# The low halves of 18 weight panels computed on GpSimd instead of VectorE

## What is computed

```python
def swiglu(x, w_in, w_out):
    g, u = jnp.split(x @ w_in, 2, axis=-1)
    return (jax.nn.silu(g) * u) @ w_out

def hgrn2_mixer(x, w_in, gnorm_w, w_out, lb):
    q, f_pre, i_in, g = jnp.split(x @ w_in, ...)     # 1024 -> 4096
    ...                                              # gated recurrence by blocks of 16
    return o.reshape(B, S, D_MODEL) @ w_out
# diff_attention: x @ w_in is 1024 -> 3072; pool_mixer: 1024 -> 1024;
# hybrid_mixer: 1024 -> 5656; recurrent_mixer: 1024 -> 2048
```

## Time and profile before

| what | before |
|---|---|
| median of 3 runs | 3395.22 us (3392.09 to 3395.25) |
| the profiled execution | 3390.7 us |
| its span, first to last instruction | 3389.0 us |
| mean granted TensorE clock | 0.968 |
| TensorE busy | 3157.4 us (93%) |
| VectorE busy | 2276.0 us (67%) |
| ScalarE busy | 1741.2 us (51%) |
| GpSimd busy | 183.0 us (5%) |

### The profile page before, as it was taken

The page is one execution under the profiler, slowest core; times in us unless marked ns, Lnnn a source line. Parts: engine busy times, 40 slices in busy tenths (PEclk is TensorE's granted clock), DMA queues, the critical chain, the costliest instruction groups (busy, mean ns, idle before and its releaser), DMA issues.

```text
span 3389.0 us, 43988 instructions
## 1 busy us (share of the span) xinstructions
PE 3157.4 (93%) x17560; PEld 2714.7 (80%) x17560; DVE 2276.0 (67%) x2669; ACT 1741.2 (51%) x2101; POOL 183.0 (5%) x147
## 2 busy tenths in 40 slices
PE   8998999998899998899998899999897999997798
PEld 7876888887688887788886788888675888886687
DVE  7667585857476776575857667575865675857674
ACT  5555554645454654554645555554443554644553
POOL 1010000001000101001000000101000101000000
PEclk9998999999899999999998999999897999998899
DMA  5542354553245454354553245454430454553353
GB/s 205 192 155 105 121 193 178 183 190 137 87 172 189 173 187 162 121 190 162 199 187 124 100 149 191 170 190 170 149 137 1 154 195 162 199 187 119 117 187 124
DMA packets 74056, 534.72 MB, mean 158 GB/s; under 512 B 8336, under 2 KB 8464, under 8 KB 9104
## 3 DMA queue, kind: packets, MB, share of 16 engines
q1 hardware_dynamic: 73872, 532.07, 44.1%
HBM read 530.99 MB, written 1.05 MB: 157 GB/s over the span
## 4 chain that ended last, share of the span: by engine, by line
PE 74%; DVE 12%; ACT 6%; DVEq 5%; issue 1%; DMA 0%; ACTq 0%; SPq 0%
PE pp L1840 35%; PE pp L1841 17%; PE pm L1840 8%; PE pp L1963 4%; PE pm L1841 4%; DVE wlo L1667 3%; ACT whi L1512 2%; DVE h L1695 2%; DVEq L1694 2%; PE pp L1862 2%; DVE mix L1693 1%; ACT corr L1569 1%; DVEq L375 1%; DVE mix L1792 1%; PE pp L1864 1%
## 5 line engine op out<-in xcount | busy, mean ns | idle before, releaser
L1840 PE MATMUL pp<-xs,whi 128*128 128x512 f32 x4912 | 1741.9, 400 | 27.7 <-DVE tsum L1712 25.0
L1667 DVE TENSOR_TENSOR wlo<-raw,whi 128x2048 fp32r<-128x2048 f32 x485 | 1110.3, 2292 | 461.2 <-ACT whi L1512 461.1
L1841 PE MATMUL pp<-xs,wlo 128*128 128x256 f32 x4912 | 1376.9, 280 | 0.0
L1840 PEld LDWEIGHTS pp<-xs,whi 128*128 128x128 f32 x4912 | 933.3, 190 | 256.4 <-issue 39.6
L1512 ACT ACTIVATE whi<-raw 128x2048 fp32r<-128x2048 f32 x485 | 925.0, 1911 | 289.6 <-DMA raw<-weights 288.8
L1841 PEld LDWEIGHTS pp<-xs,wlo 128*128 128x128 f32 x4912 | 936.0, 191 | 0.7 <-issue 0.2
L1569 ACT ACTIVATE corr<-pp 128x512 f32<-128x512 f32 x356 | 211.5, 594 | 561.4 <-PE pp L1841 535.8
L1712 DVE TENSOR_TENSOR tsum<-pp,corr 128x512 f32<-128x512 f32 x343 | 236.5, 690 | 314.9 <-ACT corr L1569 314.2
L1840 PE MATMUL pp<-hs,whi 128*128 128x512 f32 x1120 | 395.8, 394 | 0.0
L1840 PE MATMUL pm<-hs,whi 128*128 128x512 f32 x1120 | 393.0, 392 | 0.0
L1488 POOL TENSOR_TENSOR mix<-mix 128x512 f32<-128x512 f32 (+1 forms) x126 | 178.8, 1419 | 3189.2 <-ACT mix L1538 2914.9
(11 more groups left out here) (339 smaller groups left out, 2464.8 us busy)
## 6 DMA issues: line engine op xcount, KB each, us to landing
raw<-weights SPq DMA_DIRECT2D x505, 1024.0 KB, 4.8
h<-x_by_feature SPq DMA_DIRECT2D x1, 1024.0 KB, 6.9
out<-h SPq DMA_DIRECT2D x4, 256.0 KB, 2.5
vec<-vectors SPq DMA_DIRECT2D x1, 264.0 KB, 7.3
lamrow<-diff_lambda SPq DMA_DIRECT2D x1, 128.0 KB, 14.7
skiprow<-ssm_d SPq DMA_DIRECT2D x1, 8.0 KB, 14.6
```

The costliest lines, as they stand in the source:

```text
L1667: v.tensor_tensor(wlo[:, slot, :], raw[:, slot, :], whi[:, slot, :].bitcast(F32), ALU.subtract).then_inc(sem("weights_lo"), 1)
L1840: mm(bank, whi[:, slot, c:c + P], x_k, start=start, stop=False)
L1841: return mm(bank[:, 0:T], wlo[:, slot, c:c + P], x_k[:, 0:T], start=False, stop=stop)
```

## The change

GpSimd makes the low part of panels 5, 8, 11, 14 and 17 of each mixer, counted from 0 at its first panel, as far as they belong to an input projection. That is 18 panels: four in each HGRN mixer (5, 8, 11, 14), three in differential attention (5, 8, 11), five in the hybrid mixer (5, 8, 11, 14, 17), two in the RG-LRU mixer (5 and 8), none in the pooling mixer. VectorE skips these; TensorE waits for a semaphore of their own. GpSimd's loop over the sublayers is unrolled, and the panels' subtractions stand between the sublayer's first four adds and its last three. Each waits only for `weights_hi` of its panel.

```diff
+                elif s["kind"] != FFN and not seg.wide and g - s["segs"][0].g0 in (5, 8, 11, 14, 17):
+                    pool_low_panels.add(g)
...
+        def low_parts_of(pe, g):
+
+            if g in pool_low_panels:
+                pe.wait_ge(sem("pool_weights_lo"), pool_lows_before[g] + 1)
+            else:
+                pe.wait_ge(sem("weights_lo"), lows_before[g] + 1)
...
-            with pool.Fori(0, len(subs)) as n:
+            for s in subs:
+                n = s["n"]
                 for k in (2, 4, 6):
                     pool.wait_ge(sem("squares_ready"), 6 * n + k // 2)
                     add(sq[:, 0:2, :], sq[:, k:k + 2, :])
                     pool.drain()
                 add(sq[:, 0, :], sq[:, 1, :]).then_inc(sem("squares_added"), 1)
+                for seg in s["segs"]:
+                    for g in range(seg.g0, seg.g0 + seg.panels):
+                        if g in pool_low_panels:
+                            slot = g % SLOTS
+                            pool.wait_ge(sem("weights_hi"), splits_before[g] + 1)
+                            nc.gpsimd.tensor_tensor(wlo[:, slot, :], raw[:, slot, :], whi[:, slot, :].bitcast(F32), ALU.subtract
+                                                    ).then_inc(sem("pool_weights_lo"), 1)
...
             def split(g):
 
-                if g >= panels or g in whole_panels:
+                if g >= panels or g in whole_panels or g in pool_low_panels:
                     return
...
             def first_pair(seg, fill):
 
                 g = seg.g0
-                pe.wait_ge(sem("weights_lo"), splits_before[g] + 2)
+                low_parts_of(pe, g)
+                low_parts_of(pe, g + 1)
...
             def panel_product(g, half, r, between=None):
-                pe.wait_ge(sem("weights_lo"), splits_before[g] + 1)
+                low_parts_of(pe, g)
```

More of the change, by code:

```diff
@@ L95, in build @@
     splits_before, whole_panels = [], set()
+    lows_before, pool_lows_before, pool_low_panels = [], [], set()
     log1ps = hgrns = seconds = 0
@@ L111, in build @@
                 splits_before.append(g - len(whole_panels))
+                lows_before.append(splits_before[-1] - len(pool_low_panels))
+                pool_lows_before.append(len(pool_low_panels))
                 if seg.whole:
                     whole_panels.add(g)
+                elif s["kind"] != FFN and not seg.wide and g - s["segs"][0].g0 in (5, 8, 11, 14, 17):
+                    pool_low_panels.add(g)
             panels += seg.panels
@@ L351, in pe_rec @@
             pe.wait_ge(sem("panel_out"), seg.r0)
-            pe.wait_ge(sem("weights_lo"), splits_before[seg.g0] + 1)
+            low_parts_of(pe, seg.g0)
             w = seg.g0 % SLOTS
@@ L1905, in down_products @@
                 for p in range(seg.wide):
-                    pe.wait_ge(sem("weights_lo"), splits_before[seg.g0 + p] + 1)
+                    low_parts_of(pe, seg.g0 + p)
                     wide_wait(p)
```

## The result

The changed kernel takes 3441.31 us (median of 4 runs, 3437.95 to 3443.89) where the kernel before takes 3395.23 (4 runs): the ratio is 1.0135, with a 95% interval of 1.0123 to 1.0147. It is slower by 46 us, where 37 were forecast; the time lies inside the range. Its profiled execution took 3439.4 us, with a span of 3437.7, 48.7 longer than the span of before. One of the ten executions of the kernel before that e5b to e8b are compared with took 3977.45 us at a mean clock of 0.74; the ratios leave it out, and without it their kernel before takes 3396.21 us instead of 3396.72.

A forecast was written before the change was run, and what follows sets the result against it. TensorE was taken to bound the whole kernel, but VectorE's chains to set the pace in the touched mixers. The places sum to +39.9 us, forecast as +37 on the median, 3432 us, range 3408 to 3450.

The forecast's parts named there:

- the engines shut each other out for a whole instruction: GpSimd's subtraction and VectorE's instructions with two SBUF inputs exclude each other, VectorE held from T + 0.1 to T + 4.7.
- Rival 1: No shutting out: VectorE keeps its pace beside GpSimd, the kernel gains 28 us, 3367 us; chance 10%.
- Rival 2: Shut out, but VectorE's pauses take the lateness and only saturated places lose: 3400 to 3412 us; chance 10%.
- rival 3: GpSimd much slower with fp32r output, 6.9 us an operation, 39 us on top, 3471 us; chance 9%.
- the price of one low part: One GpSimd subtraction of 2048 columns, extended from the rows of its adds: 4.6 us, bounds 4.4 and 5.1.
- HGRN 1: First HGRN mixer: grows some 8.5 us, panel 5 costing 2.5 and panels 8, 11 and 14 2.0 each.
- HGRN 2: Second HGRN mixer: the same places and sizes as the first, some 8.5 us.
- Attention: Differential attention: panel 5 costs 2.5 us, panels 8 and 11 2.0 each, 6.5 in all.
- Hybrid: Hybrid mixer: panel 5 costs 2.5 us, panel 8 3.9, panels 11 and 14 5.0 together, panel 17 nothing.
- RG-LRU: RG-LRU mixer: panels 5 and 8, where VectorE is saturated, cost 2.5 us each, 5.0 in all.
- Between the mixers: Feed-forward stretches, outside the four kinds of mixer touched, were to grow not at all: 0 us.
- the clock: Longer gaps can lower TensorE's granted clock; TensorE was held to have slack, so 5 us at the upper end only.

The follow-up runs named there:

- e5b: Changed kernel, but three GpSimd memsets (writes only) replace each subtraction and TensorE uses the high part for the low part; 3380.83 us, ratio 0.9960.
- e8b: Kernel before, VectorE keeping all low parts, plus 18 spare GpSimd subtractions that read two different buffers; 3475.78 us, ratio 1.0235.
- e2: Kernel before, VectorE keeping all low parts, plus 18 spare GpSimd subtractions with one buffer as both inputs; 3455.25 us, ratio 1.0171.
- e1: Changed kernel without GpSimd's subtractions: waits kept, one column set, TensorE multiplies the high part again, 18 low parts left out; 3374.67 us, ratio 0.9936.
- e9: The changed kernel once more, unaltered; 3439.47 us, ratio 1.0134 to the kernel before.
- e7b: Changed kernel, but for panel 8 of the hybrid mixer GpSimd also waits for the scans; 3437.42 us, ratio 1.0127 to the kernel before.
- e4: Changed kernel, but panel 14 of both HGRN mixers stays on VectorE; 3431.66 us, ratio 1.0104 to the kernel before.
- e10: Changed kernel with panel 14 of both HGRN mixers left on VectorE, same edit as e4, run again; 3425.29 us, ratio 1.0093 to the kernel before.
- e6b: Changed kernel with nine other panels on GpSimd, each started when VectorE ends its work ahead of a pause; 3373.85 us, ratio 0.9936 to the kernel before.

## Why the prediction was right, step by step, and where its sizes were off

**Right: the engines shut each other out for a whole instruction.** This decided the sign, and rested on one row of 1.36 us. L876's 4.86 us, L1687's 5.02 us at p = 2, the unchanged `tsum`, and the holds in e2 and e8 show it. The forecast spoke of two SBUF inputs only. In attention what is held is a tensor-scalar, with one SBUF input and a column of scalars, which never took over 0.35 us before:

```profile
834.44 4.67 DVE L640 TENSOR_SCALAR mix<-mix 128x256 f32<-128x256 f32 x1
```

Rival 1 (no shutting out) falls by these rows. e1 shows what it would have brought: -22.6 us, where its sum had 28. Rival 2 (swallowed) falls by the growth in every mixer; rival 3 (6.9 us an instruction) by the 4.6 us measured.

**Right: the price of one low part,** 4.6 us forecast and 4.606 in the median, from the slope of two adds a quarter of its size and less.

**The sum, place by place,** forecast against the lateness table (after, e9):
- HGRN 1: 8.5 against 13.7 and 13.2. Inside (after), panel 5 is 2.3 (2.5 forecast), panel 8 is 1.8 (2.0), panel 11 is 2.3 (2.0) and panel 14, by e7b, 1.5 (2.0): the holds were sized well, and without the fall of the clock their sum is e7b's 7.3. On top come 4.1 of clock in after and e9, and 1.7 at the out projection in after, e9 and e7b, which e4 and e10 lack here. These 1.7 are the clock again: L1020 follows a gap of 2.14 us there in every trace of the table, that of before (L1008) included, and takes 2.07 us at a granted clock of 0.52 (after, 375.0 to 378.5). In HGRN 2 it is e4, e10 and also e1, in which GpSimd subtracts nothing, that have 1.6 to 1.7 at this place. So this share came by chance and hangs on no hold.
- HGRN 2: 8.5 against 10.5 and 10.5. Without panel 14, e10 shows 7.2 and e4 11.5.
- Attention: 6.5 against 4.6 and 4.5. That is about 0.7 us less a place; why was not followed up.
- Hybrid: up to 2520 12.2 and 12.0 against 11.4: to the columns 5.8 and 5.9 (forecast 6.4), of which panel 8 is 3.3 (3.9) by e7; behind them 6.4 and 6.1 for panels 11 and 14 (5.0). Panel 17 holds nothing, as forecast: L1221 keeps 0.68 us beside it. From 2520 to 2680 come 2.2 and 5.3 more. e1, in which GpSimd does nothing of the kind, gains lateness there too (3.8), and the execution of before has a granted clock of 0.87 in that stretch where e1, for the same matmuls (2500.0 to 2664.0), has 0.83. No subtraction of GpSimd's lies in that stretch, so this part is no hold. In the table it runs from -1.1 (e10) to 6.7 (e6b): so much executions differ here without any hold.
- RG-LRU: 5.0 against 4.2 and 3.8.
- Between the mixers: 0 against 1.4. The other kernels show 0.9 to 1.6 from 930 to 1800, e1, without the subtractions, the most. It comes at the pooling mixer's out projection, where the granted clock is 0.54 in after (1392.5 to 1396.0) and 1.00 in before (1372.0 to 1376.0); no hold lies near.

**The step that was mis-sized: the clock.** The prediction said "TensorE has slack there, so I add 5 at the upper end only". TensorE has no slack behind the last gap of an HGRN mixer: the sums and the out projection follow one another at TensorE's pace. There a spell at 1.2 GHz costs 4.1 us (HGRN 1) and 4.3 (HGRN 2, e4 against e10). In HGRN 1 it was panel 14 that opened the gap; in HGRN 2 e4's gap is there without panel 14. The span is 9 us over the sum of 39.9, and the two HGRN mixers make up 7.2 of them (5.2 and 2.0 in after), with a price of at most 10.9 for the two panels 14, where the sum has 4.0. The other differences nearly cancel: attention and RG-LRU were too high by 3, the hybrid mixer up to 2520 and the stretch ahead of HGRN 2 too low by 2; the 2.2 behind 2520 lie in no hold. That the forecast of the median is 9 short as well is a coincidence: 3 us were taken off that did not come, and the medians grew by 46 where the profiled span grew by 49.

**A deduction that did not come.** 3 us were taken off because "some places will let one VectorE instruction more through before GpSimd starts". In the HGRN rows GpSimd starts 0.04 us ahead of L876 after all, since VectorE reaches L876 just when the rounding ends. Of the 18, one took 6.12 us, so there GpSimd waited; the other 17 took 4.51 to 4.63 us and were in first.

**What stays open.** Why the clock fell after gaps of 2.33 and 2.43 us and not after one of 2.48 the traces don't tell. In HGRN 2 e4 and e10 differ by 4.3 us, 11.5 against 7.2, for the same code. The price of panel 14 is therefore in part that of a chance: 14.2 us is what it came to in four runs each of e9 and e10, and 9.7 to 11.7 in the changed kernel and e4. That the fall follows from the gap is argued from a few executions; no run lengthened the gap alone.

## What to carry to other kernels

Before an element-wise operation is moved to GpSimd, look at what VectorE does during it: where it was at work on two SBUF inputs here, the whole of GpSimd's longer duration was added to VectorE's path, and 2.3 us saved cost 4.6. The same operation, started by a wait at the head of one of VectorE's own pauses, held nothing at eight of nine places, and nine so placed gained as much (22.9 us) as leaving eighteen low parts out altogether (22.6). And when a wait on a chain grows, count what TensorE does behind the gap at half the clock as a term of the sum, above all where the work behind it has no slack.

## What the runs showed of the hardware that was not expected

- GpSimd's duration depends on which buffers it reads: a subtraction of 2048 columns held VectorE 3.4 us with one buffer as both inputs (e2) and 4.4 us with two, the rest being equal (e8). Where GpSimd went first, as before the scans of the hybrid mixer, its record is 3.60 us in e2 and 4.49 in e8.
- A memset of 2048 columns on GpSimd (1.81 us) leaves VectorE's two-input instructions alone (0.42 us) but holds a tensor-scalar instruction (1.10 us instead of 0.42), in e5. A subtraction holds a tensor-scalar as well (L640, 4.67 us in the changed kernel).
- The same code with the same gap, 2.3 to 2.5 us, was followed by some 10 us at a granted clock of 0.50 to 0.54 in two profiled executions and by none in a third. At the out projection of HGRN 1 a gap of 2.14 us was followed by 3.4 us at 0.50 in e9 and by none in e4.
